# Third FFN: 512 columns for the high halves and 256 for the low in its first two units

## The reference

```python
h = rmsnorm_2(x, norm_ffn[l])
ug = causal_dwconv(h @ w_ffn_in[l], conv_w[l], conv_b[l])
u, g = jnp.split(ug, 2, axis=-1)
x = x + (jax.nn.silu(g) * u) @ w_ffn_out[l]
```

## Time and profile before

| | |
|---|---|
| median of 3 runs | 852.61 us |
| profiled execution | 852.38 us |
| its span in the profile | 850.50 us |
| TensorE (PE) busy | 838.4 us, 99% |
| weight loads (PEld) busy | 740.3 us, 87% |
| VectorE (DVE) busy | 646.8 us, 76% |
| ScalarE (ACT) busy | 442.6 us, 52% |
| GpSimd (POOL) busy | 88.4 us, 10% |
| HBM traffic | 155.9 MB |

### The profile page before, as it was taken

The page is one execution under the profiler, slowest core; times in us unless marked ns, Lnnn a source line. Parts: engine busy times, 40 slices in busy tenths (PEclk is TensorE's granted clock), DMA queues, the critical chain, the costliest instruction groups (busy, mean ns, idle before and its releaser), DMA issues.

```text
span 850.5 us, 13840 instructions
## 1 busy us (share of the span) xinstructions
PE 838.4 (99%) x5335; PEld 740.3 (87%) x5335; DVE 646.8 (76%) x818; ACT 442.6 (52%) x571; POOL 88.4 (10%) x70
## 2 busy tenths in 40 slices
PE   8999999999999999999999999999999999999996
PEld 6888888888998888888888899999998988888895
DVE  5786766768967586676676868999665798998997
ACT  6555444546434554544444636476435655665663
POOL 1100000005450300000000300410003000000002
PEclk9999999999999999999999999999999999999999
DMA  8876566455843468566556664757446456466541
GB/s 254 313 234 211 182 197 210 154 194 175 237 166 117 148 225 279 188 222 199 196 179 167 145 187 116 187 151 200 149 149 198 149 185 211 148 200 216 176 173 49
DMA packets 119234, 158.10 MB, mean 186 GB/s; under 512 B 4573, under 2 KB 104333, under 8 KB 119069
## 3 DMA queue, kind: packets, MB, share of 16 engines
q1 hardware_dynamic: 116460, 150.93, 56.4%
q0 software_dynamic: 1488, 5.34, 1.8%
q10 hardware_dynamic: 1248, 1.32, 0.5%
HBM read 154.79 MB, written 1.07 MB: 183 GB/s over the span
## 4 chain that ended last, share of the span: by engine, by line
PE 98%; DMA 1%; DVE 1%; ACTq 0%; ACT 0%; issue 0%
PE wk L1743 30%; PE acc L1865 19%; PE wk L1712 18%; PE wk L1751 15%; PE acc L1842 6%; PE wk L2188 1%; PE acc L2158 1%; PE acc L2170 1%; PE acc L1759 1%; DMA x<-in_x 1%; PE acc L1878 1%; PE wk L2243 0%; PE wk L2245 0%; PE acc L1712 0%; PE acc L2206 0%; PE acc L2057 0%
## 5 line engine op out<-in xcount | busy, mean ns | idle before, releaser
L1743 PE MATMUL wk<-xhl,w_hi 128*128 128x512 f32 x1104 | 268.8, 391 | 0.0
L996 DVE TENSOR_TENSOR w_lo<-raw,w_hi 128x2048 fp32r<-128x2048 f32 x83 | 189.9, 2288 | 64.0 <-ACT w_hi L473 62.9
L1743 PEld LDWEIGHTS wk<-xhl,w_hi 128*128 128x128 f32 x1104 | 202.5, 188 | 38.9 <-issue 0.2
L473 ACT ACTIVATE w_hi<-raw 128x2048 fp32r<-128x2048 f32 x83 | 158.0, 1903 | 0.0
L1751 PEld LDWEIGHTS wk<-xhl,w_lo 128*128 128x128 f32 x1104 | 145.4, 191 | 7.9
L1751 PE MATMUL wk<-xhl,w_lo 128*128 128x256 f32 x1104 | 148.1, 283 | 0.0
L979 DVE TENSOR_TENSOR w_lo<-raw,w_hi 128x2048 fp32r<-128x2048 f32 x49 | 113.6, 2320 | 21.4 <-ACT w_hi L466 21.2
L466 ACT ACTIVATE w_hi<-raw 128x2048 fp32r<-128x2048 f32 x53 | 100.8, 1910 | 47.0 <-PE wk L1712 31.8
L1712 PE MATMUL wk<-xhl,w_hi 128*128 128x256 f32 x672 | 120.5, 286 | 0.0
L1865 PE MATMUL acc<-w_hi,hhl 128*128 128x512 f32 x480 | 119.4, 391 | 0.0
L1712 PEld LDWEIGHTS wk<-xhl,w_hi 128*128 128x128 f32 x672 | 102.4, 191 | 0.8 <-issue 0.3
(11 more groups left out here) (272 smaller groups left out, 963.1 us busy)
## 6 DMA issues: line engine op xcount, KB each, us to landing
raw<-in_ffn_w SPq DMA_DIRECT2D x65, 1024.0 KB, 5.3
raw<-in_w_in SPq DMA_DIRECT2D x26, 1024.0 KB, 7.3
raw<-in_w_ffn_in SPq DMA_DIRECT2D x22, 1024.0 KB, 5.1
raw<-in_w_ffn_out SPq DMA_DIRECT2D x11, 1024.0 KB, 4.9
raw<-in_w_out SPq DMA_DIRECT2D x8, 1024.0 KB, 4.9
arena<-bias_scratch POOLq DMA_DIRECT2D x4, 512.0 KB, 6.1
raw<-in_cmp_w_k SPq DMA_DIRECT2D x2, 1024.0 KB, 5.6
raw<-in_cmp_w_v SPq DMA_DIRECT2D x2, 1024.0 KB, 7.0
```

Of the source, the lines that this page charges most:

```text
L473: nc.scalar.activation(w_hi[:, s], raw[:, s], ACT.Copy).then_inc(hi_done, 1)
L996: nc.vector.tensor_tensor(w_lo[:, s], raw[:, s], w_hi[:, s].bitcast(F32), ALU.subtract) \
L1743: mm = nc.tensor.matmul(bank, wh[:, c, cols], xhl[:, c].rearrange("p n t -> p (n t)"), start=c == 0, stop=False, skip_group_check=True)
```

## The change

In the third FFN the first two units also take the second form, 512 columns for the high weights and 256 for the low.

- TensorE: U_FFN3 into banks 0 and 1 of `wk`, U_FFN3+1 into banks 2 and 3 (`first_unit(s0, n, True)` and `spread_unit`, as the second FFN has them). The zeroing matmul (L1805) goes. The root's two transposes write `acc[:, 0]` in place of `wk[:, 3, T:]`. Step 1 now waits for `a_sum` and `b_sum` in place of `a_out` and `b_out`.
- ScalarE: two copies of the second halves to `part3`: of U_FFN3 ahead of the split of U_FFN3+2, of U_FFN3+1 ahead of the split of U_FFN3+3.
- VectorE: two additions. That for a stands right behind the root (`rstd_rows`) and ahead of the low half of U_FFN3+2; the scaling keeps its place behind `rstd_copy`. That for b stands with its scaling where the scaling was, behind a's taps.
- The counts of `a_low`, `b_low`, `a_sum` and `b_sum` shift by one.

```diff
@@ ScalarE, ffn3_step @@
                 if first:
+                    act.wait_ge(unit_done, U_FFN3 + 1)
+                    nc.scalar.activation(k_n(part3, 2), wk[:, 0:2, T:2 * T], ACT.Copy).then_inc(a_low, 1)
                     hi(U_FFN3 + 2)
+                    act.wait_ge(unit_done, U_FFN3 + 2)
+                    act.wait_ge(a_sum, n0 + 1)
+                    nc.scalar.activation(k_n(part3, 2), wk[:, 2:4, T:2 * T], ACT.Copy).then_inc(b_low, 1)
                     hi(U_FFN3 + 3)
@@ VectorE @@
-            def summed(i, bank, dst, low_sem, sum_sem, out_sem):
-                dve.wait_ge(low_sem, i + 2 * FI)
+            def summed(i, bank, dst, low_sem, sum_sem, out_sem, scales=True):
+                dve.wait_ge(low_sem, i + (2 * FI + 1))
                 nc.vector.tensor_tensor(k_n(dst, 2), wk[:, bank:bank + 2, 0:T], k_n(part3, 2), ALU.add) \
                     .then_inc(sum_sem, 1)
-                dve.wait_ge(sum_sem, i + 2 * FI)
+                dve.wait_ge(sum_sem, i + (2 * FI + 1))
+                if scales:
+                    times_root(i, dst, out_sem)
+
+            def times_root(i, dst, out_sem):
                 nc.vector.tensor_tensor(k_n(dst, 2), k_n(dst, 2), bcast(rstd_b[:], 2), ALU.mult).then_inc(out_sem, 1)
                 dve.wait_ge(out_sem, i + (2 * FI + 1))
@@ VectorE, ffn3_step @@
                 if first:
                     rstd_rows(4)
+                    summed(0, 0, a_s, a_low, a_sum, a_out, scales=False)
                     lo_after_pool(base + 2)
-                    rstd_copy(4, wk[:, 3, T:2 * T])
+                    rstd_copy(4, acc[:, 0, 0:T])
...
+                elif first:
+                    times_root(0, a_s, a_out)
                 else:
-                    scaled(i, 0, a_s, base + 1 if first else i * 3 + base, a_out)
+                    scaled(i, 0, a_s, i * 3 + base, a_out)
...
                 taps(i, 0, a_s, conv_a, 22)
-                if form == "middle":
+                if not last:
                     summed(i, 2, b_s, b_low, b_sum, b_out)
@@ TensorE, ffn @@
-                elif parted:
-                    pe.wait_ge(lo_done, base + 1)
-                    first_unit(s0, n, parted).then_inc(unit_done, 1)
-                    spread_unit(s1, 1, base + 2).then_inc(unit_done, 1)
                 else:
                     pe.wait_ge(lo_done, base + 1)
-                    first_unit(s0, n, parted).then_inc(unit_done, 1)
-                    pe.wait_ge(lo_done, base + 2)
-                    col_tile(s1, 0, wk[:, 2, 0:T])
-                    spread(n, wk[:, 3, T:])
-                    col_tile(s1, 1, wk[:, 2, T:2 * T]).then_inc(unit_done, 1)
+                    first_unit(s0, n, True).then_inc(unit_done, 1)
+                    spread_unit(s1, 1, base + 2).then_inc(unit_done, 1)
...
-                    step(1, opens=True, **({} if parted else {"free": (a_out, b_out), "n_free": n0}))
+                    step(1, opens=True)
```

More of the change, by code:

```diff
@@ L771, in ffn3_step @@
                         act.wait_ge(unit_done, i * 3 + U_FFN3)
-                        act.wait_ge(b_sum, i + (n0 - 1))
+                        act.wait_ge(b_sum, i + n0)
                         nc.scalar.activation(k_n(part3, 2), wk[:, 0:2, T:2 * T], ACT.Copy).then_inc(a_low, 1)
@@ L781, in ffn3_step @@
                     act.wait_ge(unit_done, i * 3 + (U_FFN3 + 1))
-                    act.wait_ge(a_sum, i + n0)
+                    act.wait_ge(a_sum, i + (n0 + 1))
                     nc.scalar.activation(k_n(part3, 2), wk[:, 2:4, T:2 * T], ACT.Copy).then_inc(b_low, 1)
@@ L1606, in ffn3_step @@
                 taps(i, 0, a_s, conv_a, 22)
-                if form == "middle":
+                if not last:
                     summed(i, 2, b_s, b_low, b_sum, b_out)
                 else:
-                    scaled(i, 2, b_s, base + 2 if first else i * 3 + (base + 1), b_out)
+                    scaled(i, 2, b_s, i * 3 + (base + 1), b_out)
                 dve.wait_ge(tanh_out, i + (n0 + 1))
@@ L1939, in spread_unit, with step @@
                     return mm
-                def step(i, opens=False, spreads=False, whole=False, free=(a_sum, b_sum), n_free=n0 if parted else n0 - 1):
+                def step(i, opens=False, spreads=False, whole=False, free=(a_sum, b_sum), n_free=n0):
                     a_free, b_free = free
```

## The result

The changed kernel takes 856.78 us in the median of 6 runs (856.59 to 857.31); the kernel before, run beside it, takes 852.51 (852.32 to 853.32). The ratio is 1.005, with a 95% interval of 1.004 to 1.006. The prediction was 856.9 us, slower, with a range of 854.8 to 858.0.

A forecast was written before the change was run, and what follows sets the result against it. TensorE was taken to bound the kernel, with hardly any lead over ScalarE and VectorE at U_FFN3+6. Its 0.53 us saving and waits of 1.54, 0.87, 0.48 and 1.9 gave 4.3 us more: 856.9 us, range 854.8 to 858.0.

The forecast's parts named there:

- TensorE's own work: Third FFN's opening on TensorE: 12.26 us as in the second FFN, in place of 12.79, so 0.53 us saved.
- ScalarE's wait: ScalarE's second copy waits for the second unit's end; the split of U_FFN3+3 behind it starts at 670.65, not 664.78.
- VectorE.: VectorE behind that split: low half of U_FFN3+3 3.59 us late, extra addition 0.74 more, then everything 4.33 late.
- TensorE's waits: TensorE waits 1.54, 0.87 and 0.48 us from step 1's second unit on, then 1.9 at U_FFN3+6; none later.
- Absorbed by the loop: Rival: TensorE has more lead at U_FFN3+6, only the first step's 2.4 us of waits stay; 855.0 us; chance 0.08.
- Everything covered: Rival: at step 1's second unit nothing is late, TensorE keeps its 0.53 us; 852.1 us, no change; chance 0.05.
- The clock: Rival: clock falls to half in a new wait, one 5.57 us unit at half speed; up to 862.5 us; chance 0.03.
- A later wait missed: Rival: an overlooked later wait (loads, the sum of a) adds 1 to 2 us, up to 858.9; chance 0.06.
- The sum −0.53 + 1.54 + 0.87 + 0.48 + 1.9: TensorE's saving plus its four waits up to U_FFN3+6, 4.3 us in all, matching the ScalarE and VectorE chain's lateness.
- the 1.54: TensorE's wait in step 1, after ending U_FFN3+2 at 675.52, for the sum of b, done at 677.06: 1.54 us.

The follow-up runs named there:

- e6: Kernel before the change, with ScalarE's split of each w2 unit moved ahead of the copy of h of the step before: 852.41 us, ratio 0.9999.
- e4: Changed kernel with both splits ahead of the copies, VectorE's low half of U_FFN3+2 ahead of a's sum, and w2 splits ahead of h's copy: 851.75 us.
- e3: Kernel before the change, with only one wait added: ScalarE waits for the end of U_FFN3+1 before splitting U_FFN3+3: 856.15 us.
- e1: Changed kernel with ScalarE's split of U_FFN3+3 moved ahead of the second copy: 854.55 us, ratio to the kernel before 1.0023.
- e2: Changed kernel with VectorE's sum of b moved ahead of the low half of U_FFN3+3, into VectorE's idle time: 856.05 us.
- e5: Changed kernel with only ScalarE's split of each w2 unit moved ahead of the copy of h of the step before: 855.84 us.

## Why the prediction was right

**TensorE's own work** was costed at −0.53 us from the second FFN's opening. The changed kernel's opening lasts 669.91 − 657.65 = 12.26 us, the predicted figure, and the 0.50 us between the profiled executions of e6 and e4 agree with it. The zeroing matmul took 0.04 of the 0.53 (657.69 to 657.73 before), which leaves 0.49 for the 32 groups. The Trainium skill, page "TensorE: Matmul & The Clock Gate", section "Back-to-back issue gap", gives N/2.4 + 2.5 ns for the isolated gap of a warm matmul; the prediction's estimate from it was 0.08. The trace does not agree with that estimate, and the rows were the right choice. The saving reaches the result through ScalarE: the second copy waits for the end of U_FFN3+1, so the split behind it starts earlier by what TensorE saved. e3 has neither the saving nor the copy, and its split starts 12.99 us after the opening (657.99 to 670.98), against 12.96 in the changed kernel (657.65 to 670.61): the 0.53 saved and the 0.50 of the copy cancel.

**ScalarE's wait.** Forecast: second copy at 670.15, split of U_FFN3+3 at 670.65. Measured: 670.11 and 670.61. e3 shows that this wait alone is enough for 3.7 of the 4.3. e1 shows that the split's place behind the copy does it, and that 2.1 stay when only this is mended.

**VectorE.** The low half of U_FFN3+3 was put at 672.59 and is at 672.62; the sum of b at 676.38 and is at 676.40; the low half of U_FFN3+4 at 683.55 and is at 683.54. The extra addition was put at 0.74 of the lateness. e2, which hides it, gives back 0.73.

**TensorE's waits.** Forecast by starts: U_FFN3+3 at 677.06, the `w2` unit at 683.51, its low passes at 685.84, U_FFN3+6 at 696.84. Measured: 677.14, 683.56, 685.89, 696.88, each within 0.08. The idle times in the brackets are shorter than the forecast waits (0.58 for 0.87, 0.19 for 0.48, 1.50 for 1.9), because the profile puts the end of a matmul later than its successor can start: in the old kernel the low pass from 679.70 "ends" at 681.78, and the next matmul starts at 681.62. The starts are the safer reading. Set against the old kernel's 5.57, 5.57, 1.84 and 9.16 us between the same starts, they give the terms of the sum: −0.57, 1.66, 0.85, 0.49 and 1.83, in all 4.26. (Of the −0.57, 0.04 is the opening's own earlier start.) The forecast had −0.53, 1.54, 0.87, 0.48 and 1.9. Two slips in it are small: 677.06 + 5.57 is 682.63 and not 682.65, and its last wait is 696.84 − 695.0 = 1.84.

**The rivals.** *Absorbed by the loop* (855.0 us): no; the wait at U_FFN3+6 is there, and e2 and e5 show that the time follows the chain and not the first wait. *Everything covered* (852.1 us): its condition was that the split of U_FFN3+3 and the sum of b are in time by 675.5. In e1 both are, and the kernel is still slower by 2.1, so the condition was named too weakly: the whole chain has to be in time, as in e4, which reaches 851.75. *The clock:* no; 1.00 in every stretch of the table. *A later wait missed:* none.

The sum −0.53 + 1.54 + 0.87 + 0.48 + 1.9 must not be read as a list of prices. Its entries are not independent: e2 shows that removing the 1.54 gives 0.73. The sum held because it was carried to the point where the lateness is largest, U_FFN3+6, and there, as the prediction itself says, it had to agree with the lateness of the ScalarE and VectorE chain. Had it stopped at the end of step 1, it would have been 1.9 short. Its entries are off by up to 0.12 and cancel. That is hardly luck, since each wait ends at a time that the feeding chain fixes.

## What to carry to other kernels

An instruction that waits for the bounding engine must not stand in a queue ahead of work that the bounding engine will want: put the splits, copies and loads that are free to go before the one that waits. When the bounding engine shows no idle time, still measure its lead at each hand-over; where the lead is near zero, every addition on the feeding chain costs its full length, even though that engine is busy only three quarters of the time. And a gap in the trace is not a price: ask where the lateness is largest, and cost the change there.

## What the runs showed that was not expected

After a wait TensorE's first group takes a little longer. The 16 high matmuls that start at 677.14, behind a wait, take 3.77 us to the next group (680.91), where those at 669.91 take 3.66 (673.57). The eight low matmuls behind the wait at 685.89 take 1.97 (e2: 685.26 to 687.24, 1.98), where the old kernel's took 1.81 (683.46 to 685.27). That is 0.1 to 0.16 us per wait at a granted clock of 1.00; why, no run here shows. It mostly vanished in the next wait, which ends at a time fixed by the other engines. Behind the last wait it stays: the lateness is 4.26 at U_FFN3+6 and 4.36 at the end.
